# Moving two cache copies behind the recurrence's outputs in a hybrid decoder step

## The reference, cut to what matters

```python
def nsa_sample(q, kc, vc, ks, vs, kw, vw, ng, page_table, ck_cmp, cv_cmp, ck_slc, cv_slc, ck_win, cv_win, ...):
    ...
    wk = jnp.concatenate([ck_win, kw], axis=1)
    wv = jnp.concatenate([cv_win, vw], axis=1)
    ...
    return o.reshape(n, ds, D_Q), wk[:, -wb:], wv[:, -wb:]
```

## Time and profile before

| | |
|---|---|
| median of 3 runs | 1878.54 us (1878.17 to 1879.04) |
| the profiled execution | 1879.48 us, its span 1877.7 us |
| TensorE busy | 97%, granted clock 0.991 on average |
| VectorE, ScalarE, GpSimd busy | 80%, 60%, 13% |
| DMA | 514 MB, 274 GB/s on average |

### The profile page before, as it was taken

How to read it: one execution, slowest core, us unless ns; L and a number is a source line. 1 busy time by engine, 2 the same in 40 slices (tenths; PEclk the granted TensorE clock), 3 DMA queues, 4 the chain that set the end, 5 groups by cost and what they waited for, 6 DMA issues and landing times.

```text
span 1877.7 us, 27455 instructions
## 1 busy us (share of the span) xinstructions
PE 1830.7 (97%) x9813; PEld 1502.2 (80%) x9813; DVE 1502.5 (80%) x1754; ACT 1129.8 (60%) x1126; POOL 245.0 (13%) x259
## 2 busy tenths in 40 slices
PE   7999999999999999999999999999999999999998
PEld 5898988787768677888888888888888888888886
DVE  6865876644367458999999999999999999999995
ACT  5335544442432346767776776776776777677674
POOL 0040000012330133100110010010011001001000
PEclk9999999999999999999999999999999999999999
DMA  5074221123355249999999999999999999999993
GB/s 227 8 245 168 68 76 51 46 84 96 113 151 196 91 154 370 374 379 383 373 377 388 376 369 390 381 366 385 387 370 373 394 368 371 388 386 369 388 368 106
DMA packets 76747, 514.23 MB, mean 274 GB/s; under 512 B 10744, under 2 KB 31296, under 8 KB 50800
## 3 DMA queue, kind: packets, MB, share of 16 engines
q1 hardware_dynamic: 58944, 454.19, 61.5%
q0 software_dynamic: 17584, 58.51, 11.6%
q10 hardware_dynamic: 144, 0.55, 0.1%
HBM read 490.36 MB, written 28.24 MB: 276 GB/s over the span
## 4 chain that ended last, share of the span: by engine, by line
PE 75%; issue 8%; DVE 7%; ACT 6%; DMA 3%; ACTq 0%; DVEq 0%; POOL 0%; SPq 0%; POOLq 0%
PE bank L1153 26%; PE bank L1171 14%; PE bank L703 6%; PE bank L755 5%; PE bank L630 3%; ACT qT_rounded L1558 3%; PE bank L603 3%; PE bank L1002 3%; PE bank L1135 2%; PE bank L1129 1%; DMA ring<-in_w_exp 1%; PE bank L977 1%; DVE slab L2303 1%; DVE slab L2306 1%; PE bank L1145 1%
## 5 line engine op out<-in xcount | busy, mean ns | idle before, releaser
L2256 DVE TENSOR_TENSOR ring_rounded<-ring,wide_rounded 128x2048 fp32r<-128x2048 f32 x192 | 431.4, 2288 | 50.7 <-ACT wide_rounded L1558 50.3
L1153 PE MATMUL bank<-ring_rounded,slab_rounded 128*128 128x512 f32 x1024 | 400.7, 391 | 0.0
L1558 ACT ACTIVATE wide_rounded<-ring 128x2048 fp32r<-128x2048 f32 x192 | 359.8, 1908 | 10.4 <-PE bank L1153 8.8
L1153 PE MATMUL bank<-xn_rounded,slab_rounded 128*128 128x512 f32 x1024 | 327.5, 391 | 0.0
L2256 DVE TENSOR_TENSOR ring_rounded<-ring,xn_rounded 128x2048 fp32r<-128x2048 f32 x128 | 292.9, 2288 | 16.6 <-ACT xn_rounded L1558 16.6
L1171 PE MATMUL bank<-wide_rounded,slab_rounded 128*128 128x512 f32 x768 | 258.9, 398 | 0.0
L1153 PE MATMUL bank<-wide_rounded,slab_rounded 128*128 128x512 f32 x768 | 247.2, 389 | 0.0
L1558 ACT ACTIVATE xn_rounded<-ring 128x2048 fp32r<-128x2048 f32 x128 | 244.0, 1906 | 0.0
L1153 PEld LDWEIGHTS bank<-ring_rounded,slab_rounded 128*128 128x128 f32 x1024 | 192.6, 188 | 41.5
L1153 PEld LDWEIGHTS bank<-xn_rounded,slab_rounded 128*128 128x128 f32 x1024 | 193.1, 189 | 40.4 <-issue 0.8
L2483 POOL DMA_INDIRECT out_y<-slab,small x32 | 85.1, 2659 | 1001.8 <-ACT slab L1633 1001.8
(11 more groups left out here) (463 smaller groups left out, 2989.3 us busy)
## 6 DMA issues: line engine op xcount, KB each, us to landing
ring<-in_w_exp SPq DMA_DIRECT2D x192, 2048.0 KB, 10.8
ring<-in_w_blk SPq DMA_DIRECT2D x40, 512.0 KB, 3.6
slab<-in_w_tok SPq DMA_DIRECT2D x4, 1304.0 KB, 15.4
ring<-in_w SPq DMA_DIRECT2D x8, 512.0 KB, 3.7
ring<-in_w_out SPq DMA_DIRECT2D x2, 2048.0 KB, 13.4
xn<-in_xT SPq DMA_DIRECT2D x4, 520.0 KB, 8.1
ring<-in_k_cmp SPq DMA_DIRECT2D x32, 64.0 KB, 3.5
ring<-in_k_cmp POOLq DMA_DIRECT2D x32, 64.0 KB, 2.7
```

Of the source, the lines that this page charges most:

```text
L1153: r = mm(bank[:, c, :], a[:, 4 * h + k, :], w[:, k, :], start=False, stop=h == 1 and k == 3 and x == 2)
L1558: fn(WH[(2 * c + h) % 6], ring[:, half_of(c, h)], ACT.Copy).then_inc(S["wh_ready"], 1)
L2256: v.tensor_tensor(ring_r[:, half_of(c, h)], ring[:, half_of(c, h)], WHf[(2 * c + h) % 6], ALU.subtract)\
```

## The change

The two copies of cached rows into the window outputs move in GpSimd's list from behind the first cache pages to behind the three outputs of the recurrence. Nothing else is edited.

```diff
@@ -2403,8 +2403,6 @@
             second_pages("xsk", d["k_cmp"], S["k_pages_in_pool"])
-            dma(d["o_kwin"][:, :, 0:WIN - 1], d["k_win"][:, :, 1:WIN]).then_inc(S["outs_done"], 16)
-            dma(d["o_vwin"][:, 0:WIN - 1, :], d["v_win"][:, 1:WIN, :]).then_inc(S["outs_done"], 16)
             pool.wait_ge(S["qk_dve"], TT)
             dma(d["o_kwin"][:, :, WIN - 1], kT[:, 2, NPR:NT], allow_slow_non_contiguous=True).then_inc(S["outs_done"], 16)
 
@@ -2412,6 +2410,8 @@
             dma(d["o_h"], hout).then_inc(S["outs_done"], 16)
             dma(d["o_pconv"], pconv).then_inc(S["outs_done"], 16)
             dma(d["o_sconv"], xps).then_inc(S["outs_done"], 16)
+            dma(d["o_kwin"][:, :, 0:WIN - 1], d["k_win"][:, :, 1:WIN]).then_inc(S["outs_done"], 16)
+            dma(d["o_vwin"][:, 0:WIN - 1, :], d["v_win"][:, 1:WIN, :]).then_inc(S["outs_done"], 16)
             pool.wait_ge(S["kv_out"], 16 * (TT + 1))
             dma(kvraw[:, 0:2, 0:384], d["w2"].rearrange("p (v c) -> p v c", v=2)).then_inc(S["w2_in"], 16)
```

## The result

The changed kernel takes 1875.84 us in the median of 20 runs, the kernel before 1878.67 of 20: a ratio of 0.9984 with a 95% interval of 0.9977 to 0.9991. So it is faster by 2.8 us, 0.16%, clear of zero, where 1.0 us slower was forecast. The profiled execution went from 1879.48 to 1876.45 us, its span from 1877.7 to 1874.8.

A forecast was written before the change was run, and what follows sets the result against it. TensorE, busy 97% of the span, was taken to bound the kernel; saving 7.4 us at the old place and losing 8.4 at the new gave +1.0, 1879.5 us in the median, range 1871 to 1883.5.

The forecast's parts named there:

- A: Saving at 145 to 236 us once the copies leave the old place: 7.4 us, bounds 5.8 and 9.1.
- TensorE's pace: Gate products from 151.04 to 182.02 us would run every 13.25 us without waits, saving 4.5 us.
- The wait at 228.81: TensorE's wait of 2.20 us for `turned(0)` would shrink to 0.9, saving 1.3 us.
- B: Cost at 252 to 276 us, where the moved copies meet a block load: 8.4 us, bounds 0 and 11.
- The same meeting, so the landing is 252.0 + 20.2 = 272.2.: At the new place the block load would land 20.2 us behind the first copy's issue, as at the old one.
- The 0.7 us that I took off: Deduction from the new place's cost because the load, following the copies sooner, may get more packets through before the V copy.
- rival 1: At the new place the load shares packets and lands before the V copy starts, costing nothing; 1871.1 us, chance 0.22.
- The half clock: Behind TensorE's long wait at the new place its clock would drop, costing 1.5 of the 2.4 us seen earlier.
- The 1.1 us of new waiting for VectorE: Behind the late landing, VectorE handles the block's lower half before the maxima the next weights need, adding 1.1 us.
- Rival 2: At the new place the load lands one V-copy piece later, about 274.3 or after; loss over 3.8 us, 1883, chance 0.19.
- Rival 3: The column write of 1024 single elements, not the copies, holds the load at 145.5; slower by 8, chance 0.03.
- TensorE gains or loses passes to the end whole: Behind 280 us TensorE's progress releases every load, so its gain or loss reaches the end undiminished.

The follow-up runs named there:

- e9: The kernel before, unedited, profiled once more; that execution took 1879.65 us.
- e10: The kernel before, unedited, a second further look at its clock; that execution took 1879.76 us.
- e2: Against the changed kernel, both copies stand ahead of the three recurrence outputs, 1.6 us sooner; 1879.85 us, ratio 1.0004.
- e3: Against the changed kernel, same place, V copy split with slowest dimension 16, over 16 engines in smaller pieces; 1873.53 us, ratio 0.9973.
- e5: Against the kernel before, only the K copy moves to the new place, the V copy stays; 1873.63 us, ratio 0.9968.
- e8: The changed kernel, unedited, measured and profiled once more; 1875.85 us, ratio 0.9984.
- e1: Against the kernel before, both window copies are left out, so 511 of 512 output rows are not written; 1873.61 us, ratio 0.9967.
- e4: Against the changed kernel, both copies move behind the value cache pages, issued at 427.5; 1873.79 us, ratio 0.9974.
- e6: Only the V copy moves to the new place, the K copy stays behind the key cache pages; 1876.79 us, ratio 0.9990.
- e7: Against the kernel before, nothing moved, V copy over 16 engines in pieces of 16 KB; 1873.30 us, ratio 0.9969.
- e11: Against the changed kernel, copies ahead of the recurrence's outputs and V copy over 16 engines; 1876.11 us, ratio 0.9983.

## Why the prediction was wrong

**A, held against this profile.** Forecast -7.4 us at 267 us, measured 267.28 - 274.62 = -7.3. TensorE's pace: L570 at 177.71 instead of 182.02, 4.3 us (4.5). The wait at 228.81: 0.94 left (0.9). VectorE's end of the last scan released GpSimd 6.85 us earlier (6.8). The new waiting for VectorE: 0.9 (0.8). That the sum fits to 0.1 us is in part luck, for the profile that A was read from was a slow one up to here. In e9 and e10 the stall is a little shorter and the slow stretch half as long; they are 2.3 and 1.9 us ahead of the first profile at 236 us, 0.9 and 0.5 of it from the stall and 1.4 from the clock. Against these two, A was 5.0 and 5.4 us, and 0.3 us of it was the clock, where 1.6 was forecast.

**B, the step that failed:** "The same meeting, so the landing is 252.0 + 20.2 = 272.2." The load was issued 1.4 us behind the copies, as worked out, but landed at 264.0. I took the distance from the copies to the landing as fixed. It depends on when the load comes. From the first copy's issue to the landing it was 20.8 us at a distance of 3.1 (e2), 20.3 at 3.2 (e10), 19.4 at 2.6 (e9), 20.2 at 2.4 (the kernel before), and 12.1 at 1.4 (the changed kernel). The 0.7 us that I took off for just this was the term, and it should have been 8. The prediction's own figures had it: 4.7 us without a packet and 4.2 us for 8 packets on each engine put the last packet at 253.3 + 8.9 = 262.2, only 0.9 us behind the start of the V copy that rival 1 reckons with (261.3), while the same sum for the load of 145.5 gives 154.4, 2.1 us behind 152.3.

Behind the landing the forecast was nearly right. With the load caught (e2), ScalarE waits 8.0 us and TensorE 5.3, and TensorE goes on 1.6 us behind the landing at 270.8 (1.5). The half clock then costs 1.8 us (1.5): TensorE is 2.2 us ahead at 272.42 and 0.4 a round later. The 1.1 us of new waiting for VectorE did not come. That is 7.1 us in all for e2, against 8.4.

**The term that was missing.** Only one load was priced. The next one, of 262.6, met the V copy, landed at 275.3, and made the 1.38 us of TensorE at 281. The distance to the kernel before went from -7.3 to -5.6 us there. B was 1.7 us instead of 8.4. e3 and e5 free this load, and TensorE's wait is gone in both.

**Rival 1** (the meeting is cheap) had the mechanism, by the forecast's own sign: the load of 253 lands in under 12 us. q1 was served packet by packet in time, though again not in the first 4 us. The argument against it, that delay, was no argument, as the sum above shows. Its time of 1871.1 was 4.7 us too low: it had no second load, and it took A whole. Rival 2 needed a landing of 274.3 for the load of 253 and is out. Rival 3, the column write, is out by the changed kernel itself: the write is still there, issued at 143.31, and the load of 145.7 lands in 4.6 us.

**"TensorE gains or loses passes to the end whole":** a single profile does not show it. The first profile of the changed kernel is 5.6 us ahead at 283 us, 4.3 at the first L755 (416.8 against 421.1), and 2.9 at the expert stage; the second is 5.9 and 6.3 at these last two. All three executions of the kernel before ended within 0.3 us of one another, though two of them were some 2 us ahead of the third at 287. Where the slow stretches fall differs between executions, as the windows above show. Over all kernels it does hold. Here is the lead over the first profile of the kernel before, by TensorE's values product that stands there at 288.85, and the gain of the median over that of the kernel before measured beside it:

| kernel | stands at | lead | gain of the median |
|---|---|---|---|
| changed (e8) | 283.21 (282.99) | 5.6 (5.9) | 2.8 (2.9) |
| e1 | 281.23 | 7.6 | 5.0 |
| e2 | 288.39 | 0.5 | -1.3 |
| e3 | 281.43 | 7.4 | 5.0 |
| e4 | 281.81 | 7.0 | 4.8 |
| e5 | 281.18 | 7.7 | 5.1 |
| e6 | 284.79 | 4.1 | 2.0 |
| e7 | 281.34 | 7.5 | 5.4 |
| e11 | 283.20 | 5.6 | 3.3 |

The gain is the lead less 1.7 to 3.0 us throughout, and e9 and e10 stand at 286.52 and 286.93, which is 2.3 and 1.9 us of lead for the same kernel. So the first profile of the kernel before was some 2 us behind its kind at this point, and what an edit gains by 285 us does reach the median. That two more executions stand for the usual run is argued, not shown. Of the changed kernel, 5.6 less 1.9 to 2.3 leaves 3.3 to 3.7, and 2.8 was measured; what takes the rest stays open.

## What to carry to other kernels

A bulk copy that no one waits for is priced by the loads issued in the 20 us behind it, all of them, and each by its distance to the copy: list them with issue time, landing and the moment their reader asks. A distance that shifts by 1.6 us can be worth more (4.0 us, e2 against the changed kernel) than moving the copy by 109 us (2.8). First give the copy a slowest dimension that uses all 16 engines, and smaller pieces with it; here this took TensorE's stall away where it stood (e7), though not in every place (e11), and moving the copy to a stretch without loads did as well (e4). And before a slow stretch of the clock goes into a sum, see in a second profile of the same kernel whether it comes again.

## What the runs showed that I had not expected

- A load that meets q0 filled by the K copy gets no packet for 4 to 5 us (none in 4.7 us in the earlier trace rows, none in 4.0 in the changed kernel), behind the V copy alone none for 2 to 3.5 us (e5, e6), and without the copies the first comes some 1.2 us behind the issue (the load of 145.7 in the changed kernel). From then on it shares q0's engines (38 packets of q0 and 36 of q1 in 259:260 of the changed kernel). The Trainium skill (DMA: Bandwidth & Descriptors, Queues, rings and completion order) has the sharing packet by packet; no run here shows what the delay is.
- Two copies in a row held a load issued 2.4 to 3.2 us behind them for 16.8 to 17.7 us, one issued 1.4 us behind for 10.7; behind one copy alone it was 8.7 to 14.4.
- ScalarE could lose 4.9 to 5.2 us at 152 us (e5, e7) without TensorE noticing; 10.5, 10.8 and 11.4 us (e9, e10, the first profile) cost 3.4, 3.8 and 4.3 of TensorE's pace.
- TensorE fell to 1.2 GHz behind the same wait of 2.2 us for 6.8 us in one execution and for 3.4 in two others.
